# Dilated mixer: where the scores of a piece stand in a slot, and where VectorE takes their slope and maximum

## The reference, cut to what matters

```
proj = h @ w_in                     # q, k, v of 3 groups, 16 heads of 64
for gi, (window, dil) in enumerate(((128, 1), (512, 4), (2048, 16))):
    ...
    scores = einsum(q, k) * 64 ** -0.5                # prompt: blocks of 128 with the block before
    scores = where(valid, scores + bias, -inf)        # bias = -slope(head) * dil * distance
    p, lse = softmax_lse(scores)                      # row maximum, exp, sum
    o = einsum(p, v)
    ...                                               # samples: 129 gathered keys of the past and of the step
o = sum_gi softmax(lse)_gi * o_gi
x = x + o @ w_out
```

## Time and profile before

| | us |
|---|---|
| median of 3 runs | 2387.17 |
| lowest and highest | 2384.52, 2390.51 |
| profiled execution: its own time | 2386.47 |
| profiled execution: span | 2384.7 |
| mean granted clock of TensorE | 0.964 of full speed |
| busy in the span: PE, DVE, ACT, POOL | 91%, 58%, 31%, 18% |
| the dilated mixer | about 1189.5 to 1967 |

### The profile page before, as it was taken

One profiled execution on the slowest core, in us unless ns is written; L12 is line 12 of the kernel. 1 busy time (PEld: TensorE's weight loads), 2 busy tenths in 40 slices (PEclk: granted clock), 3 DMA queues, 4 the chain that ended last, 5 costly groups with the idle time before them and its releaser, 6 DMA issues.

```text
span 2384.7 us, 41702 instructions
## 1 busy us (share of the span) xinstructions
PE 2180.5 (91%) x17512; PEld 2053.1 (86%) x17512; DVE 1380.2 (58%) x2061; ACT 736.0 (31%) x1408; POOL 437.3 (18%) x287
## 2 busy tenths in 40 slices
PE   7998896897789999999998998999898879999997
PEld 7988775676688999999998887897897859999997
DVE  4886776876755544344565565665656557343444
ACT  4332323445343322122313422322332334122221
POOL 1000322321121100000035334344424500000000
PEclk9998997997999999999999999999999999999998
DMA  4225666863333787777748678568757956777874
GB/s 166 71 71 177 242 240 212 293 214 109 102 115 124 256 280 250 262 267 256 256 150 287 241 236 303 174 212 297 242 182 241 315 183 212 264 265 247 281 248 179
DMA packets 282910, 519.93 MB, mean 218 GB/s; under 512 B 17776, under 2 KB 253664, under 8 KB 278880
## 3 DMA queue, kind: packets, MB, share of 16 engines
q1 hardware_dynamic: 271408, 324.44, 41.6%
q10 hardware_dynamic: 5888, 177.91, 20.6%
q0 software_dynamic: 5440, 15.08, 1.7%
HBM read 483.76 MB, written 210.80 MB: 291 GB/s over the span
## 4 chain that ended last, share of the span: by engine, by line
PE 61%; DVE 12%; issue 9%; DMA 9%; ACT 4%; POOL 3%; SPq 1%; DVEq 0%; ACTq 0%; POOLq 0%
PE gp L2309 33%; PE gp L2873 13%; PE gp L2462 4%; DMA uk<-in_dil_k 4%; PE gp L2657 2%; DVE cacc L1574 2%; DMA vs<-in_dil_v 2%; DMA decay<-tmp_a_row 2%; POOL uq L2972 2%; PE mp L2748 1%; POOL at_f L2932 1%; DVE sc_t L2131 1%; ACT w_hi L1021 1%; PE mp L2823 1%; DVE hs_t L1731 1%
## 5 line engine op out<-in xcount | busy, mean ns | idle before, releaser
L2873 PE MATMUL gp<-a_hi,w_hi 128*128 128x272 f32 x1152 | 348.7, 304 | 2.0 <-DVE q_t L2057 2.0
L2873 PE MATMUL gp<-a_lo,w_hi 128*128 128x272 f32 x1152 | 333.3, 290 | 0.0
L2873 PE MATMUL gp<-a_hi,w_lo 128*128 128x272 f32 x1152 | 331.9, 289 | 0.0
L2309 PE MATMUL gp<-a_hi,w_hi 128*128 128x272 f32 x1456 | 306.2, 292 | 23.4 <-DVE w_lo L1497 12.1
L2972 POOL TENSOR_TENSOR uq<-uq,uk 128x1024 f32<-128x1024 f32 x96 | 256.8, 2681 | 287.4 <-DMA uk<-in_dil_k 287.1
L2309 PE MATMUL gp<-a_lo,w_hi 128*128 128x272 f32 x1456 | 303.0, 290 | 0.0
L2309 PE MATMUL gp<-a_hi,w_lo 128*128 128x272 f32 x1456 | 302.0, 289 | 0.0
L2309 PEld LDWEIGHTS gp<-a_hi,w_hi 128*128 128x128 f32 x1456 | 231.5, 190 | 26.3 <-DVE cin L1563 13.0
L2873 PEld LDWEIGHTS gp<-a_hi,w_hi 128*128 128x128 f32 x1152 | 218.3, 190 | 26.4 <-issue 23.0
L2309 PEld LDWEIGHTS gp<-a_hi,w_lo 128*128 128x128 f32 x1456 | 230.5, 190 | 0.0
L2309 PEld LDWEIGHTS gp<-a_lo,w_hi 128*128 128x128 f32 x1456 | 229.1, 190 | 0.0
(11 more groups left out here) (382 smaller groups left out, 4182.9 us busy)
## 6 DMA issues: line engine op xcount, KB each, us to landing
out_dil_ks<-in_dil_k ACTq DMA_DIRECT2D x32, 2044.0 KB
out_dil_vs<-in_dil_v ACTq DMA_DIRECT2D x32, 2044.0 KB
uq<-tmp_rows SPq DMA_DIRECT2D x96, 512.0 KB, 6.1
w_raw<-in_odd_w_in SPq DMA_DIRECT2D x36, 1024.0 KB, 7.9
vs<-in_dil_v SPq DMA_DIRECT2D x67, 512.0 KB, 7.2
w_raw<-in_w_up SPq DMA_DIRECT2D x32, 1024.0 KB, 8.2
w_raw<-in_w_down SPq DMA_DIRECT2D x32, 1024.0 KB, 8.0
uk<-in_dil_k SPq DMA_DIRECT2D x64, 512.0 KB, 7.4
```

Source lines behind the costliest of these rows:

```text
L2309: m = nc.tensor.matmul(gp[:, c, h, 0:HALF], w[:, sl, k, c * P:(c + 1) * P], x[:, k, h * HALF:(h + 1) * HALF], start=n < 2, stop=n >= 46)
L2873: m = nc.tensor.matmul(out, w[:, k, n * P:(n + 1) * P], x[:, k, h * HALF:(h + 1) * HALF], start=k == 0 and j == 0, stop=k == last_k and j ...
```

## The change

Three edits of order; no instruction is added, removed or resized.
- On PE `score1` of a pair goes from part 7 to part 5 of its even slot.
- On PE `turn1` goes from part 5 to part 4.
- On DVE `score1` of piece z goes from the start of iteration z+1 to iteration z, behind the drain of the slot's first half and ahead of `item_out`.

```diff
@@ VectorE @@
                 if 1 <= z <= N_SLOTS and ODD[i][0] != "o":
                     drain(i, (z - 1) % 2, 1)
-                if z - 1 in PIECE:
-                    score1(PIECE[z - 1])
                 for kind, qd, x in SMALL_AT.get((z - 1, 7), ()):
                     small_out(kind, qd, x)
...
                 if z < N_SLOTS and ODD[z // 2][0] != "o":
                     drain(z // 2, z % 2, 0)
+                if z in PIECE:
+                    score1(PIECE[z])
                 for n, qd, g, b in ITEM_AT.get(z - 1, ()):
                     item_out(n, qd, g, b)
@@ TensorE, beside(z, part) @@
-                if part == 5 and z - 1 in PIECE:
+                if part == 4 and z - 1 in PIECE:
                     turn1(PIECE[z - 1])
-                if part == 7 and PIECE.get(z, 1) % 2 == 0:
+                if part == 5 and PIECE.get(z, 1) % 2 == 0:
                     score1(PIECE[z])
```

## The result

| | before | changed |
|---|---|---|
| median, us | 2390.51 (5 runs) | 2411.35 (5 runs) |
| lowest and highest | 2384.52, 2400.05 | 2407.19, 2414.36 |
| profiled execution: its own time, span | 2386.47, 2384.7 | 2414.36, 2412.6 |
| mean granted clock | 0.964 | 0.956 |

The change makes the kernel slower: ratio 1.0083, 95% interval 1.0063 to 1.0104. The forecast was 2399 with a range to 2410: the direction was right, the size, +11.7 against +20.8, about half of what came, and 2411.35 lies above the range. Of the 12.4 us by which 2399 was missed 3.3 are the kernel before, whose median is 2390.51 over five runs and was 2387.17 over the three that the forecast started from.

The account below looks back on a forecast made before the run. PE held 61% of the chain, with turn waits of 22.5 us and load waits of 21.0. Quad 0 +0.5, quad 1 +4.7, quad 2 +4.2, quad 3 +2.8, tail -0.5: +11.7 on 2386.47, forecast 2399, range 2376 to 2410.

Parts of the forecast that it names:

- turn waits: PE waiting for a piece's exponential before its turn: 22.5 us, near zero before the tail, 5 to 7 us in it.
- first gate: Slots 30/31, 51 to 53, 71 to 73: piece between drain and item sums delays the `vs` load, +1.4 us each.
- wait at L2781: PE's wait for the last item sum in slots 37 and 57: 2.4 us instead of 1.0, +1.4 each.
- quad 0: Turn stalls of odd slots given back in even slots, at the copied piece: +0.5 us, between -4 and +3.
- Scores in part 5 ... nothing: On PE, the same 4 to 8 score matmuls two parts earlier: taken as 0 us.
- The term left out of the sum: the clock: PE at half clock after longer waits: some 3 us left to the range, 3 to 6 in "More than the sum".
- Quad 1: Slot 30 +1.2, first gate +1.4, slot 33 +1.2, slot 35 -0.5, slot 37 +1.4: +4.7 us.
- Quads 2 and 3: Same places as in quad 1, with second gates at +0.7 each: +4.2 us in quad 2, +2.8 in quad 3.
- The tail: Last slots, where pieces form a chain of their own: -0.5 us, between 0 and -2.
- Built-for gain: Rival, faster: loads have slack or gates open earlier; fully -15.3 us gives 2372, half gives 2379; chance 0.18.
- One for one: Rival, no change: gate losses matched by gains in quad 0's odd slots and `x_t` drains; +0.7 us, 2388; chance 0.2.
- More than the sum: Rival, slower: high ends of the terms plus the clock's 3 to 6 us; +21 us, 2408; chance 0.12.

Follow-up runs that it names:

- items away from both places: Kernel before, item sums of iterations 12, 30, 50, 70 ahead of the `v_st` drain, those of 36, 56, 76 behind two `x_t` additions of next slot: 2367.27 us.
- The fill: Changed kernel with needless TensorE matmuls in part 2 of slots 37, 57 and 77, just ahead of the wait for `x_t`: 2408.21 us, ratio 1.0066.
- the gates out of the way: The change's three edits on top of items away from both places, scores of slots 36, 56, 76 kept in part 7: 2378.54 us, ratio 0.9947.

## Why the prediction was right in kind and short in size

**Right.** The turn waits are gone outside the tail, and 4.3 us of them left in it, a little under the 5 to 7 said. The waits for `vs` are 30.8 us, where "some 30" stood. The first gate pays the piece's 1.4 us between drain and sums, and slot 31 grew by 1.55. The wait at L2781 is 2.40 us instead of 1.02 in slots 37 and 57. In quad 0 the waits moved from turns to the copied piece: +0.9 us up to slot 27 in the changed kernel, and the change in quad 0 alone is 1.0004. That exchange was the prediction's reading, and it is shown. A part of it runs over the clock, which the prediction did not have in this quad: in slots 0 to 19 PE's idle time fell from 12.0 to 8.7 us, and its busy time rose from 145.0 to 149.3 at a clock of 0.97 instead of 1.00. DMA's empty stretch at the first gate grew as the sign said, but by 4 us instead of 1.4.

**The term that failed first: "Scores in part 5 ... nothing".** I priced these matmuls by what waits for them and not by what stands behind them on PE. In slots 36, 56 and 76 that is the last two products, for which DVE's additions wait, then `w_lo`, then the first addition of the next slot, for which PE waits. It cost 1.3 us, and 1.6 more because `w_lo` fell behind POOL's multiplication. For slots 37 and 57 together I had 2.8 us; 11.5 came (36 to 39 and 56 to 59), and with the scores of these slots in part 7 it is 2.2. Of the 6.8 us of slots 36 to 39 2.9 are this wait, 1.4 the wait at L2781 that I had, and 2.5 matmuls at the lower clock. The wait for `x_t`, 7.5 us before and 13.1 after, does not stand in the sum at all, and the 4 to 8 matmuls of the prediction are 16 in these slots, 1.16 us long. That no instruction was added did not mean that none would take longer.

**The term left out of the sum: the clock.** It was put in the range, with 3 to 6 us in the upper rival. PE's busy time grew by 14.3 us, half of the difference, and by 10.6 in the second profile; this is the largest term that was missed. Over the runs it does not follow the sum of the idle time: before 67.1 us idle and 708.0 busy, scores in part 5 alone 69.8 and 718.0, the changed kernel 79.9 and 722.4, VectorE's edit alone 83.9 and 724.2; but with the turn back in part 5 86.0 and 715.6, and with the item sums ahead of the drain 67.6 and 722.6, items away from both places 54.2 and 709.1. So the sum of the waits does not tell what the clock costs. The fill shows the cost for one place; for the rest it is read from the windows and not tested.

**Quad 1 was under-sized.** Slots 28 to 35 grew by 8.9 us against 3.3. Slot 31 and the end of the turn waits are as forecast. Slot 30 grew by 3.6 instead of 1.2: its wait for `vs` went from 0.32 to 2.40 us (a little above the upper bound of 1.9, because the piece of slot 29 also waited 0.50 us for its turn), and its clock from 1.00 to 0.89. Slot 33 grew by 3.6 instead of 1.2: 0.70 to 2.79 us of wait and a clock of 0.86. Slot 28 was not in the sum: its `w_lo` started 0.6 us behind POOL's multiplication, 3.94 us instead of 2.29, and PE waited 1.4 us for what follows on DVE. That one is not the change's for certain: in the second profile of the changed kernel `w_lo` takes 2.29 us there and the slot is as long as before. Slots 28 to 35 take 95.1 us in it, and slots 30 and 33 are 3.6 and 3.2 us longer than before.

**Quads 2 and 3.** Slots 48 to 55 grew by 2.2 us against 2.8. Slots 68 to 75 shrank by 1.3, where I had +2.8; in the second profile they are 88.1 us, 0.7 above before. So the term is near zero in quad 3, and I can't say why. The tail is 2.8 us longer, not 0.5 shorter: slot 77 has the wait for `x_t` (2.90 to 3.37, 4.68 in the second profile) and 2.40 at L2781, which I had called covered by the turn behind it, and the lower clock. The 2.0 us in slots 40 to 47 are a wait of slot 46 at L2761 that the profile of before shows in slot 66, and not the change's; in the second profile these slots take 68.9 us, as before.

**The rivals.** Built-for gain: no; with the gates out of the way the change still cost 11 us. One for one: right for quad 0 only. "More than the sum" named the clock, gave 2408 and had a chance of 0.12; it was the nearest. Its +21 is what the medians show, but not for its reasons: it had the clock at a third of its size, nothing of `x_t`, and quad 0 at +3 where +1 came.

What stays open: which waits move the clock, and how far, and how much of the 2 to 5 us by which single stretches differ between executions of one kernel is the clock. The kernel before alone ran between 2381 and 2403 us.

## What to carry to other kernels

When work is moved forward on an in-order engine, price everything that now stands behind it, on that engine and one step further, above all where a drain or an addition feeds the engine back. Idle time in front of an instruction that waits is where other work belongs: item sums moved ahead of a drain that waits gave 16 us, while the piece moved behind that same drain cost. And a wait on TensorE can cost more than its length, since the matmuls that follow may run at the lower clock; read the busy time of the same matmuls in both profiles before adding up waits.

## What the runs showed of the hardware that I had not expected

VectorE's `w_lo` split and GpSimd's multiplication, both with two inputs in SBUF, take turns whole: the split takes 2.28 us when it starts 0.2 us ahead and 3.89 when it starts 0.6 us behind, and the multiplication 2.37 or 4.33. A shift of 1.3 us in the order was enough to turn the one into the other. The same is seen in slot 56, 3.69 us at 0.8 behind. And the lower clock cost nearly as much as all added waits together: 14.3 us of PE's busy time against 12.8 us of idle time in one profile of the changed kernel, 10.6 against 15.6 in the other.
